# A chunked recurrence on TensorE: level products in 64*64 quarters, and as block-diagonal products of two heads

## The chip, the cores and the metric

The kernel runs on one core of a Trainium2 chip. The metric is the device time of one execution in microseconds; lower is better. All data are float32.

## The reference

Two layers of a hybrid backbone over 512 tokens (256 of context, 256 latent). Each layer normalises, projects, and mixes the tokens in three ways (RWKV-7 time mixing in both directions, neighbourhood attention, chunkwise mLSTM), merges the three, and then runs a mixture of experts. The part that matters here is the recurrence of the RWKV-7 mixer. It runs for each of 8 heads (64 channels each) and each of two directions over the tokens, with a 64 x 64 state S:

```python
def step(S, inp):
    r_t, w_t, a_t, b_t, k_t, v_t = inp
    sa = jnp.einsum('bhvk,bhk->bhv', S, a_t)
    S = S * w_t[:, :, None, :] + sa[..., None] * b_t[:, :, None, :] + v_t[..., None] * k_t[:, :, None, :]
    return S, jnp.einsum('bhvk,bhk->bhv', S, r_t)
```

The context tokens come first, and their last state starts the latent tokens. The second layer needs no outputs for the context tokens, only the state.

## The kernel before

The kernel is a chain of stages, each a block of its own in which the engines' programs are written out by hand and tied by semaphores; between stages all engines meet. `stage_rwkv_scan` (from L1824) does the recurrence, once in each layer. It moves nothing by DMA.

The 512 tokens are cut into chunks of L = 64, so there are NST = 8 steps, and in a step both directions d (0 and 1) work on a chunk each. P is 128, HD is 64, and KC = 4 pairs of heads fill the 128 partitions: an even head lies on partitions 0 to 63 and an odd one on 64 to 127. Within a chunk the recurrence is solved in closed form. TensorE makes the products of the decayed rows (`matrices`, L2149), a triangular matrix per head. Its inverse is built in six levels (m = 0 to 5), each of which joins blocks twice as large: a level multiplies the inverse so far, kept as X and as its transpose, by masked factors. In a level of the kernel before (`level`, L2166), `forward` (L2184) writes psW, which DVE masks into XI (`factor`, L2070), and `backward` (L2189) writes psWT, which ACT copies to NT (`copied`, L1930). Level 5 makes only the backward half, and DVE adds the identity (`inverse`, L2075).

Every product of a level is 64 x 64 of one head. The start partition of the operands and that of the output say in which quarter of the 128 x 128 array a product lies. Two of the four head pairs swap the halves of the partitions at each odd level, so that forward and backward products use all four quarters at once:

```python
def place(hp, r, m):
    return HD - r if hp >= KC // 2 and m % 2 else r
```

For that a level is issued in two halves with a wait on `across` in between (L2199 to L2201), and `between` (L2211) puts other products there: the right side from the state (L2220) and from the values (L2227), the turning of the features to token-major order by products with the identity (L2237), and at level 0 the old state's part of the output rows (L2268).

Behind the levels of a step, TensorE makes the next step's matrices (L2159 with 128 columns, L2162 with 64), the corrections u (L2247), the product that updates the state (L2254) and the chunk's part of the output rows (L2262), and then level 0 of the next step (`step`, L2272). DVE adds the state product to the old state (L2094) and multiplies by the chunk's decay (L2100); it also applies the masks to the matrices (L2068, L2088) and makes the queries (L2057, L2061). ACT takes the exponentials of the decay sums (four a direction and step, L1915 to L1918), copies the levels, the right side (L1945), the turned features (L1939), u (L1962, L1963) and the output rows (L1969). POOL makes the other features of the next step (L1988 to L1997) and clears the buffers at the start (L2003 to L2012). The values are transposed once at the start (L2146). In the program of each engine the two directions alternate, so one direction's copies run beside the other direction's products.

## Time and profile before

| | us |
|---|---|
| median of 3 runs | 2594.16 |
| lowest and highest run | 2587.97, 2595.68 |
| the profiled execution, its time | 2594.5 |
| its span, first to last instruction | 2592.7 |
| mean granted TensorE clock, share of full speed | 0.941 |

A page of the profile gives busy times by engine. PE is TensorE's products, PEld its weight loads, DVE is VectorE, ACT ScalarE, POOL GpSimd, SP SyncE. Views of the trace give single stretches: windows (busy times between two moments), waits, groups by source line, and the timeline. In the timeline a row of several records has the start of the first, the length from there to the end of the last, and their number. A row such as `64*64 64x64` has weights on 64 rows and 64 columns of the array, and moving data of 64 partitions and 64 columns. A record's length holds the way through the array, so successive records overlap; what one costs in a series is the distance of their starts. "issue" is time in which the engine waited for nothing that the profile shows.

### The profile page before, as it was taken

What the parts mean: (1) busy time and instruction counts of PE and PEld (TensorE: products, weight loads), DVE (VectorE), ACT (ScalarE), POOL (GpSimd) and SP (SyncE); (2) the same over time, 40 slices, a digit from 0 to 9 for tenths busy, and PEclk for the clock granted to TensorE, in tenths of its full rate; (3) what the DMA queues carried; (4) which work ended last, traced back from release to release, by engine and by line L of the source; (5) the groups of instructions that cost most, each with busy time, mean ns of one, the idle gap of its engine ahead of it and who ended that gap; (6) DMA issues with size and microseconds to landing.
All of it is one profiled execution on the core that took longest, in us unless ns stands there. A gap on an engine that the chain in (4) does not pass through costs nothing. (4 is left out here: it accounts for less than half of the span.)

```text
span 2592.7 us, 49039 instructions
## 1 busy us (share of the span) xinstructions
PE 2253.1 (87%) x19954; PEld 1492.5 (58%) x19954; DVE 1159.0 (45%) x2561; ACT 707.5 (27%) x1666; POOL 392.0 (15%) x465
## 2 busy tenths in 40 slices
PE   6999989887789998899889679999888878897785
PEld 3444455547754444466556568877657767554453
DVE  3877765575542114532212563244675542522113
ACT  2011155464441002132222120024454430222220
POOL 0000000044520001132222000000133400222210
PEclk8999999999999998999999889999889999899998
DMA  9455401210016103699988733313210033999994
GB/s 379 195 211 238 168 33 43 79 46 5 4 52 259 73 1 126 263 384 388 372 348 319 297 143 113 115 67 98 98 40 4 4 128 129 355 414 390 382 377 180
DMA packets 80368, 474.39 MB, mean 183 GB/s; under 512 B 17296, under 2 KB 29200, under 8 KB 51728
## 3 DMA queue, kind: packets, MB, share of 16 engines
q1 hardware_dynamic: 55280, 419.82, 41.3%
q0 software_dynamic: 24864, 51.43, 5.2%
q8 instruction: 159, 2.61, 0.4%
q14 instruction: 65, 0.53, 0.1%
HBM read 439.99 MB, written 61.08 MB: 193 GB/s over the span
## 5 line engine op out<-in xcount | busy, mean ns | idle before, releaser
L2883 PE MATMUL xp_psG<-moe_ring,rt_xt 128*64 128x256 f32 (+1 forms) x2048 | 324.5, 402 | 42.5 <-DMA moe_ring<-in_moe 41.9
L2883 PEld LDWEIGHTS xp_psG<-moe_ring,rt_xt 128*64 128x64 f32 (+1 forms) x2048 | 225.4, 161 | 119.6 <-issue 48.2
L599 PE MATMUL win_ps<-h,win_ring 128*128 128x512 f32 x512 | 226.2, 600 | 5.4 <-PEq L292 5.4
L659 DVE SCALAR_TENSOR_TENSOR mod_acc<-ada_ring,cv_silu,mod_acc 128x512 f32<-128x512 f32 x280 | 197.9, 748 | 10.8 <-issue 0.4
L3140 DVE TENSOR_TENSOR rt_sg<-rt_sg,xp_psG 128x128 f32<-128x128 f32 x84 | 24.2, 288 | 332.3 <-ACT rt_sg L2957 332.3
L599 PEld LDWEIGHTS win_ps<-h,win_ring 128*128 128x128 f32 x512 | 97.0, 192 | 125.6 <-issue 125.6
L2904 PE MATMUL xp_psY<-moe_ring,rt_aT 128*64 128x512 f32 (+1 forms) x512 | 162.1, 602 | 4.0 <-DVE rt_aT L3147 4.0
L2192 PE MATMUL sc_ps<-sc_NT,sc_XI 64*64 64x64 f32 x2560 | 112.9, 235 | 23.3 <-issue 18.9
L1274 POOL MEMSET ml_w<- 128x1536 f32 x4 | 5.4, 1376 | 764.9 <-POOLq L973 764.9
L2187 PE MATMUL sc_ps<-sc_XI,sc_NT 64*64 64x64 f32 x2048 | 100.7, 226 | 22.1 <-issue 16.6
L2073 DVE TENSOR_TENSOR sc_XI<-sc_ps,cst 128x256 f32<-128x256 f32 x160 | 67.5, 422 | 107.9 <-PE sc_ps L2192 107.0
L2951 ACT ACTIVATE rt_xt<-xp_psT 128x512 f32<-128x512 f32 x168 | 91.0, 595 | 89.8 <-PE xp_psT L2868 89.7
L2537 DVE TENSOR_TENSOR mg_gateb<-mg_gateb,mg_psY 128x512 f32<-128x512 f32 (+1 forms) x48 | 26.6, 554 | 189.6 <-PE mg_psY L2494 184.3
L2192 PEld LDWEIGHTS sc_ps<-sc_NT,sc_XI 64*64 64x64 f32 x2560 | 89.6, 142 | 28.7 <-issue 22.4
L2757 POOL DMA_INDIRECT y_rows<-rt_y,rt_dst x56 | 56.2, 1004 | 300.5 <-PE xp_psT L2868 197.6
L2957 ACT ACTIVATE rt_sg<-xp_psG 128x128 f32<-128x128 f32 x84 | 23.4, 279 | 265.1 <-PE xp_psG L2883 265.1
L2868 PEld LDWEIGHTS xp_psT<-cst,rt_xg 128*128 128x128 f32 x512 | 58.5, 144 | 64.4 <-issue 36.8
L2187 PEld LDWEIGHTS sc_ps<-sc_XI,sc_NT 64*64 64x64 f32 x2048 | 79.1, 137 | 27.7 <-issue 17.5
L1933 ACT ACTIVATE sc_NT<-sc_ps 128x256 f32<-128x256 f32 x160 | 61.3, 384 | 120.7 <-PE sc_ps L2192 120.5
L2904 PEld LDWEIGHTS xp_psY<-moe_ring,rt_aT 128*64 128x64 f32 (+1 forms) x512 | 51.7, 153 | 69.6 <-issue 59.9
L2868 PE MATMUL xp_psT<-cst,rt_xg 128*128 128x128 f32 x512 | 70.7, 283 | 21.5 <-DMA rt_xg<-h_rows,rt_tok 21.5
L2508 PE MATMUL mg_psO<-mg_m,mg_wo 128*128 128x512 f32 (+1 forms) x256 | 83.0, 486 | 4.2 <-DVE mg_m L2541 4.2
(537 smaller groups left out, 4293.4 us busy)
## 6 DMA issues: line engine op xcount, KB each, us to landing
moe_ring<-in_moe SPq DMA_DIRECT2D x128, 1536.0 KB, 14.3
ada_ring<-in_ada SPq DMA_DIRECT2D x22, 2048.0 KB, 15.1
win_ring<-in_win SPq DMA_DIRECT2D x20, 2048.0 KB, 7.8
cb_yg<-y_rows SPq DMA_DIRECT2D x16, 1024.0 KB, 11.6
mg_ring<-in_mg SPq DMA_DIRECT2D x16, 768.0 KB, 4.4
mg_wo<-in_wo SPq DMA_DIRECT2D x2, 4096.0 KB, 14.5
pr<-y_rows SPq DMA_DIRECT2D x8, 1024.0 KB, 18.4
ml_gate_ring<-in_mg SPq DMA_DIRECT2D x12, 512.0 KB, 3.7
```

What stands on the lines that cost most here:

```text
L599: last = pe.matmul(ps[:, n % NB, first(n):T], ring[:, j % 2, c, m * P:(m + 1) * P], h[:, c, first(n):T], start=c == 0, stop=c == KD - 1)
L659: last = dve.scalar_tensor_tensor(out=acc[:, a % 2, s], in0=aring[:, a % 3, c], scalar=weight, in1=acc[:, a % 2, s], op0=ALU.mult, op1=ALU ...
L1933: act.activation(NT[d][:], psWT[d], ACT.Copy).then_inc(sem[d]["wtout"].sem, 1)
L2073: dve.tensor_tensor(XI[d][:], psW[d], level_mask(d, m), ALU.mult).then_inc(sem[d]["xi"].sem, 1)
L2187: pe.matmul(psW[d][to:to + HD, hp], wt, x, start=True, stop=True)
L2192: last = pe.matmul(out[to:to + HD], x, wt, start=True, stop=True)
L2508: last = pe.matmul(psO[:, m % 2, 0:N], wo[:, c, m * P:(m + 1) * P], mg[:, c, t0:T], start=c == 0, stop=c == KD - 1)
L2757: pool.indirect_dma_start(k.d_y[0:N * TOP_K], bass.IndirectOffsetOnAxis(ap=dst[:, column(u)], axis=0), y_rows[u % OUT], None, bounds_check ...
L2868: last = pe.transpose(psT[:, u % 2, c], xg[u % AHEAD][:, c * P:(c + 1) * P], k.cst("ident"))
L2883: last = pe.matmul(psG[at:at + m, u % 2, 0:2 * P].rearrange("p (q n) -> p q n", q=2), xt[:, u % 2, c, at:at + m], ring[:, slot, c:2 * KD:K ...
L2904: last = pe.matmul(psY[at:at + m, q], aT[:, u % 2, at:at + m], ring[:, slot, 2 * KD + 4 * q:2 * KD + 4 * q + 4], start=True, stop=True)
L2951: last = act.activation(xt[:, u % 2, q * 4:q * 4 + 4], psT[:, u % 2, q * 4:q * 4 + 4], ACT.Copy)
```

## The change

The levels from 1 up work on two heads at once. NT becomes a block-diagonal [128, 4, 2, 64]: the even head's block on partitions 0 to 63, the odd head's on 64 to 127, the rest zero, cleared once by POOL. A level is then, for each of the four pairs of heads, one product with XI as weights (128 rows, 64 columns) and NT as 128 moving columns ("back", psWT, rows 0 to 63), and one with NT as 128 x 128 weights and XI as 64 moving columns (psW, called "forward" below). Each back result is copied by two instructions, `evens` and `odds`, mostly on ACT, some on DVE (`both`, `odds_of_first`). X0 and the matrices M now hold all heads' level operands on partitions 0 to 63, so level 0 uses two quarters. The matrices are one product of 128 x 128 outputs a head, into banks of their own (psA), and are made during level 4 and not behind level 5; the second matrices (psA2) go around level 5. Token-major order comes from full transposes. The identity's part of the inverse and the old state are added by products with the identity as weights, in place of DVE adds; the sum S2 and its buffer go. ACT takes two exponentials a direction and step and not four. The products of the right side, the output rows and the state keep their shapes, and their places in the order change; `rows_of_state` now opens the sum of the output rows.

The diff, cut to its core:

```diff
-        S2 = sb("S2", [P, KC, L])
-        ex = sb("ex", [P, 3, KC, L])
+        rise = sb("rise", [P, KC, L])
+        fall = [sb(f"fall{b}", [P, KC, L + 1]) for b in range(3)]
...
-        NT = sb("NT", [P, KC, L])
-        XI = sb("XI", [P, KC, L])
-        X0 = ctx.enter_context(nc.sbuf_tensor(f"sc_X0{l}", [P, 2, KC, L], F32))
+        NT = [[pn[:, NK_T + 2 + 2 * b + d].rearrange("p (c o n) -> p c o n", c=KC, o=2) for d in range(2)] for b in range(2)]
+        XI = [pn[:, NK_T + 6, d * KC * L:(d + 1) * KC * L].rearrange("p (c n) -> p c n", c=KC) for d in range(2)]
+        X0 = ctx.enter_context(nc.sbuf_tensor(f"sc_X0{l}", [HD, 2, HEADS, L], F32))
...
-        psA = [ps[d][:, 0:2].rearrange("p b (h n) -> p b h n", n=P) for d in range(2)]
         psW = [half(d, 0, 0) for d in range(2)]
-        psWT = [half(d, 1, 0) for d in range(2)]
-        psA2 = [half(d, 3, 1) for d in range(2)]
-        psV = [ps[d][:, 2].rearrange("p (c n) -> p c n", c=KC) for d in range(2)]
-        psBK = [[half(d, 2, o) for o in range(2)] for d in range(2)]
-        psI = [ps[d][:, 0:2, 0:2 * L].rearrange("p b (c n) -> p b c n", c=KC // 2) for d in range(2)]
-        psR = [half(d, 3, 0) for d in range(2)]
+        psA2 = [ps[d][0:HD, 0].rearrange("p (h n) -> p h n", h=HEADS) for d in range(2)]
+        psWT = [ps[d][:, 1].rearrange("p (c o n) -> p c o n", c=KC, o=2) for d in range(2)]
+        psWT0 = [half(d, 1, 0) for d in range(2)]
+        psV = [ps[d][:, 1] for d in range(2)]
+        psA = [ps[d][:, 2:4].rearrange("p b (h n) -> p b h n", n=P) for d in range(2)]
+        psBK = [ps[d][:, 2] for d in range(2)]
         psU = [half(d, 2, 0) for d in range(2)]
         psS = [half(d, 2, 1) for d in range(2)]
+        psR = [half(d, 3, 0) for d in range(2)]
...
-            incl, excl, total = sums[:, :, 1 - d:1 - d + L], sums[:, :, d:d + L], sums[:, :, L - d * L]
-            act.activation(ex[d][:, 2], incl, ACT.Exp, scale=DECAY)
-            act.activation(ex[d][:, 0], incl, ACT.Exp, scale=-DECAY)
-            act.activation(ex[d][:, 1], excl, ACT.Exp, scale=-DECAY)
-            act.activation(wl[n % 3][d][:], total, ACT.Exp, scale=-DECAY).then_inc(sem[d]["exps"].sem, 1)
+            act.activation(rise[d][:], sums[:, :, 1 - d:1 - d + L], ACT.Exp, scale=DECAY)
+            act.activation(fall[n % 3][d][:], sums, ACT.Exp, scale=-DECAY).then_inc(sem[d]["exps"].sem, 1)
...
-        def copied(d, n, m):
-            w(act, d, "nn", n, m + 1)
-            act.activation(NT[d][:], psWT[d], ACT.Copy).then_inc(sem[d]["wtout"].sem, 1)
+        def evens(d, n, m):
+            w(act, d, "back", n, m + 1)
+            src = psWT0[d][0:HD] if m == 0 else psWT[d][0:HD, :, 0]
+            act.activation(NT[m % 2][d][0:HD, :, 0], src, ACT.Copy).then_inc(sem[d]["evens"].sem, 1)
+        def odds(d, n, m):
+            w(act, d, "back", n, m + 1)
+            src = psWT0[d][HD:P] if m == 0 else psWT[d][0:HD, :, 1]
+            act.activation(NT[m % 2][d][HD:P, :, 1], src, ACT.Copy).then_inc(sem[d]["odds"].sem, 1)
         def token_major(d, n):
             w(act, d, "turned", n)
-            for o in range(2):
-                last = act.activation(bk[d][:, o:HEADS:2], psBK[d][o], ACT.Copy)
-            last.then_inc(sem[d]["tok"].sem, 1)
+            act.activation(bk[d][:].rearrange("p h n -> p (h n)"), psBK[d], ACT.Copy).then_inc(sem[d]["tok"].sem, 1)
...
         def step(n):
             for m in range(1, 5):
-                for d in range(2):
-                    copied(d, n, m)
-                    if n == 0 and m == 1:
-                        exponentials(d, 1)
-                    if m == 2:
-                        right_side(d, n)
-                    if m == 4:
-                        token_major(d, n)
+                evens(0, n, m)
+                odds(0, n, m)
+                if m == 2:
+                    token_major(0, n)
+                if m == 4:
+                    right_side(1, n)
+                if n == 0 and m == 1:
+                    exponentials(0, 1)
+                    exponentials(1, 1)
+                if m % 2:
+                    evens(1, n, m)
+                    odds(1, n, m)
+                if m == 2:
+                    token_major(1, n)
+                if m == 3:
+                    right_side(0, n)
             if n + 2 < NST:
                 exponentials(0, n + 2)
+            evens(0, n, 5)
+            odds(0, n, 5)
+            evens(1, n, 5)
+            odds(1, n, 5)
...
+            if n + 1 < NST:
+                evens(0, n + 1, 0)
+                odds(0, n + 1, 0)
+                evens(1, n + 1, 0)
...
+        blocks = pn[:, NK_T + 2:NK_T + 6]
+        pool.memset(blocks, 0.0)
...
-                    pool.tensor_copy(X0[:, d], eye)
+                    pool.tensor_copy(X0[:, d], k.cst("eye", HD).unsqueeze(1).broadcast_to([HD, HEADS, L]))
...
+            w(dve, d, "seconds", n, 2)
+            first = k.cst(f"lev{d}", HD)[:, 0:L].unsqueeze(1).broadcast_to([HD, HEADS, L])
+            dve.copy_predicated(X0[:, d], first.bitcast(U32), psA2[d]).then_inc(sem[d]["xi"].sem, 1)
...
-        def inverse(d, n):
-            w(dve, d, "nn", n, 6)
-            dve.tensor_tensor(NT[d][:].rearrange("p (b c) n -> p b c n", b=2), psI[d],
-                              eye.rearrange("p (b c) n -> p b c n", b=2), ALU.add).then_inc(sem[d]["inv"].sem, 1)
+        def odds_of_first(d, n):
+            w(dve, d, "back", n)
+            dve.tensor_copy(NT[0][d][HD:P, :, 1], psWT0[d][HD:P]).then_inc(sem[d]["odds"].sem, 1)
+        def both(d, n, m):
+            w(dve, d, "back", n, m + 1)
+            dve.tensor_copy(NT[m % 2][d][0:HD, :, 0], psWT[d][0:HD, :, 0]).then_inc(sem[d]["evens"].sem, 1)
+            dve.tensor_copy(NT[m % 2][d][HD:P, :, 1], psWT[d][0:HD, :, 1]).then_inc(sem[d]["odds"].sem, 1)
...
-        def add_products(d, n):
+        def decay(d, n):
             w(dve, d, "s", n)
-            dve.tensor_tensor(S2[d][:], S[d][:], psS[d], ALU.add)
-        def decay(d, n):
-            if n in outs:
-                w(dve, d, "rows", n)
-            dve.tensor_tensor(S[d][:], S2[d][:], wl[n % 3][d][:].unsqueeze(2).broadcast_to([P, KC, L]),
+            total = fall[n % 3][d][:, :, L - d * L]
+            dve.tensor_tensor(S[d][:], psS[d], total.unsqueeze(2).broadcast_to([P, KC, L]),
                               ALU.mult).then_inc(sem[d]["state"].sem, 1)
         def step(n):
+            more = n + 1 < NST
             for m in range(1, 5):
-                for d in range(2):
-                    factor(d, n, m + 1)
-                if n + 1 < NST:
+                factor(0, n, m + 1)
+                if m % 2 == 0:
+                    both(1, n, m)
+                factor(1, n, m + 1)
+                if more:
                     (rows_query if m % 2 else key_query)((m - 1) // 2, n + 1)
-            for d in range(2):
-                inverse(d, n)
-            if n + 1 < NST:
+            if more:
+                masks(0, n + 1)
+            if more:
+                masks(1, n + 1)
                 for d in range(2):
                     first_factor(d, n + 1)
-                    masks(d, n + 1)
-            for d in range(2):
-                add_products(d, n)
-            dve.drain()
-            for d in range(2):
-                decay(d, n)
-                if n + 1 < NST:
+                odds_of_first(1, n + 1)
+                for d in range(2):
                     factor(d, n + 1, 1)
-            dve.drain()
+                for d in range(2):
+                    decay(d, n)
+                dve.drain()
...
         def matrices(d, n):
             w(pe, d, "queries", n)
             w(pe, d, "feats", n)
             if n:
-                w(pe, d, "inv", n - 1)
+                w(pe, d, "tok", n - 1)
                 w(pe, d, "rout", n - 1)
             for h, hp, r in heads:
-                o = h % 2
-                for a, q in enumerate((r, HD - r)):
-                    pe.matmul(psA[d][q:q + HD, o, hp], hat[n % 2][d][r:r + HD, hp, a],
-                              ra[n % 2][d][r:r + HD, hp].rearrange("p a n -> p (a n)"), start=True, stop=True)
+                last = pe.matmul(psA[d][:, h % 2, hp], hat[n % 2][d][r:r + HD, hp].rearrange("p a n -> p (a n)"),
+                                 ra[n % 2][d][r:r + HD, hp].rearrange("p a n -> p (a n)"), start=True, stop=True)
+            last.then_inc(sem[d]["mats"].sem, 1)
+        def second_matrices(d, n, o):
+            if o:
+                w(pe, d, "seconds", n)
+            r = o * HD
+            for hp in range(KC):
+                last = pe.matmul(psA2[d][:, 2 * hp + o], ra[n % 2][d][r:r + HD, hp, 1], hat[n % 2][d][r:r + HD, hp, 0],
+                                 start=True, stop=True)
+            last.then_inc(sem[d]["seconds"].sem, 1)
+        def first_level(d, n):
+            w(pe, d, "xi", n)
+            w(pe, d, "masked", n)
+            if n:
+                w(pe, d, "evens", n - 1, 6)
+                w(pe, d, "odds", n - 1, 6)
+            else:
+                pe.wait_ge(values_out.sem, values_out.at(NV))
             for h, hp, r in heads:
-                last = pe.matmul(psA2[d][r:r + HD, hp], ra[n % 2][d][r:r + HD, hp, 1], hat[n % 2][d][r:r + HD, hp, 0],
+                last = pe.matmul(psWT0[d][r:r + HD, hp], X0[:, d, h], M[n % 2][d][0:HD, h % 2, hp, L:P],
                                  start=True, stop=True)
-            last.then_inc(sem[d]["mats"].sem, 1)
+            last.then_inc(sem[d]["back"].sem, 1)
+            for h, hp, r in heads:
+                last = pe.matmul(psW[d][r:r + HD, hp], M[n % 2][d][0:HD, h % 2, hp, L:P], X0[:, d, h],
+                                 start=True, stop=True)
+            last.then_inc(sem[d]["nn"].sem, 1)
         def level(d, n, m):
             w(pe, d, "xi", n, m + 1)
...
+            w(pe, d, "evens", n, m)
+            w(pe, d, "odds", n, m)
+            if m == 5 and n + 1 < NST:
+                second_matrices(d, n + 1, 0)
+            wt = NT[(m - 1) % 2][d]
+            for hp in range(KC):
+                last = pe.matmul(psWT[d][0:HD, hp], XI[d][:, hp], wt[:, hp], start=True, stop=True)
+            last.then_inc(sem[d]["back"].sem, 1)
             if m < 5:
+                for hp in range(KC):
+                    last = pe.matmul(psW[d][:, hp], wt[:, hp], XI[d][:, hp], start=True, stop=True)
+                last.then_inc(sem[d]["nn"].sem, 1)
...
+        def token_major(d, n):
+            w(pe, d, "state", n)
+            for hp in range(KC):
+                last = pe.transpose(psBK[d][:, hp * P:(hp + 1) * P],
+                                    hat[n % 2][d][:, hp].rearrange("p a n -> p (a n)"), k.cst("ident"))
+            last.then_inc(sem[d]["turned"].sem, 1)
+        def side_of_state(d, n):
+            w(pe, d, "state", n)
+            pe.wait_ge(sem[d]["yout"].sem, sem[d]["yout"].at(y_read(n)))
             for h, hp, r in heads:
+                last = pe.matmul(psR[d][r:r + HD, hp], ra[n % 2][d][r:r + HD, hp, 1], S[d][r:r + HD, hp],
+                                 start=hp == 0, stop=False)
+            last.then_inc(sem[d]["rstate"].sem, 1)
+        def side_of_values(d, n):
+            w(pe, d, "rstate", n)
             for h, hp, r in heads:
+                last = pe.matmul(psR[d][r:r + HD, hp], M[n % 2][d][HD:P, h % 2, hp, L:P],
+                                 uv[HD:P, chunk(d, n), h], start=False, stop=hp == KC - 1)
+            last.then_inc(sem[d]["r"].sem, 1)
         def rows_of_state(d, n):
             if n in outs:
                 for h, hp, r in heads:
                     last = pe.matmul(psY[d][r:r + HD, hp], S[d][r:r + HD, hp], ra[n % 2][d][r:r + HD, hp, 0],
+                                     start=hp == 0, stop=False)
+                last.then_inc(sem[d]["ystate"].sem, 1)
+        def corrections(d, n):
+            w(pe, d, "rout", n)
+            if n + 1 < NST:
+                w(pe, d, "masked", n + 1)
+            else:
+                w(pe, d, "tok", n)
+            rows_of_state(d, n)
+            w(pe, d, "evens", n, 6)
+            w(pe, d, "odds", n, 6)
+            pe.matmul(psU[d], k.cst("ident"), rhs[d][:], start=True, stop=False)
+            for hp in range(KC):
+                last = pe.matmul(psU[d][:, hp], NT[1][d][:, hp], rhs[d][:, hp], start=False, stop=hp == KC - 1)
+            last.then_inc(sem[d]["u"].sem, 1)
+        def state_product(d, n):
+            w(pe, d, "uout", n)
+            if n + 1 < NST:
+                pe.matmul(psS[d], k.cst("ident"), S[d][:], start=True, stop=False)
+                for h, hp, r in heads:
+                    last = pe.matmul(psS[d][r:r + HD, hp], bk[d][:, h], uv[:, chunk(d, n), h],
+                                     start=False, stop=hp == KC - 1)
+                last.then_inc(sem[d]["s"].sem, 1)
+            if n in outs:
+                w(pe, d, "ystate", n)
+                for h, hp, r in heads:
+                    last = pe.matmul(psY[d][r:r + HD, hp], uv[:, chunk(d, n), h], M[n % 2][d][:, h % 2, hp, 0:L],
                                      start=False, stop=hp == KC - 1)
                 last.then_inc(sem[d]["rows"].sem, 1)
         def step(n):
+            for m in range(1, 5):
                 for d in range(2):
                     level(d, n, m)
+                    if m == 1:
+                        token_major(d, n)
+                    elif m == 2:
+                        side_of_state(d, n)
+                    elif m == 3:
+                        side_of_values(d, n)
+                    elif n + 1 < NST:
+                        matrices(d, n + 1)
             for d in range(2):
+                level(d, n, 5)
                 if n + 1 < NST:
+                    second_matrices(d, n + 1, 1)
+            for d in range(2):
                 corrections(d, n)
+            if n + 1 < NST:
+                for d in range(2):
+                    first_level(d, n + 1)
             for d in range(2):
                 state_product(d, n)
```

## Rows read from the trace of the kernel before

**Rows 1.** The page: its first line and the busy times of its part 1.
```profile
span 2592.7 us, 49039 instructions
...
PE 2253.1 (87%) x19954; PEld 1492.5 (58%) x19954; DVE 1159.0 (45%) x2561; ACT 707.5 (27%) x1666; POOL 392.0 (15%) x465
```

**Rows 2.** Windows: start:end, length, busy (records) of five engines, clock, DMA, GB/s.
```profile
564.20:750.95 186.75, 146.76 (x5648) 135.62 (x5648) 99.91 (x222) 83.01 (x256) 92.97 (x133) 0.94 0.02 4
577.40:750.95 173.55, 136.82 (x5476) 126.79 (x5472) 89.36 (x197) 75.68 (x235) 84.59 (x119) 0.96 0.02 4
1916.30:2099.80 183.50, 146.96 (x5392) 134.63 (x5392) 98.49 (x222) 80.97 (x248) 76.86 (x109) 0.88 0.02 4
1934.10:2099.80 165.70, 136.12 (x5228) 124.95 (x5220) 88.75 (x197) 72.37 (x223) 69.22 (x95) 0.91 0.02 4
```

**Rows 3.** Waits, first scan: who waited for what, us, times, longest.
```profile
ACT sc_NT L1933 <- PE sc_ps L2192: 57.4, 56, 2.7
DVE sc_XI L2073 <- PE sc_ps L2192: 54.8, 55, 2.6
...
PE sc_ps L2192 <- issue: 11.8, 11, 1.6
...
PE sc_ps L2187 <- issue: 9.1, 8, 1.9
```

**Rows 4.** Groups by line, first scan: count, busy, mean ns, idle before.
```profile
L2073 DVE TENSOR_TENSOR sc_XI<-sc_ps,cst 128x256 f32<-128x256 f32 x80 | 33.8, 422 | 55.2 <-PE sc_ps L2192 54.8
L1933 ACT ACTIVATE sc_NT<-sc_ps 128x256 f32<-128x256 f32 x80 | 30.6, 384 | 57.5 <-PE sc_ps L2192 57.4
```

**Rows 5.** Timeline of PE, first scan: start, length, line, shapes, count.
```profile
606.74 0.69 PE L2237 MATMUL sc_ps<-cst,sc_hat 64*64 64x64 f32 x32
```

**Rows 6.** Timeline of PE, end of the second step of the first scan.
```profile
615.57 1.06 PE L2159 MATMUL sc_ps<-sc_ra,sc_hat 64*64 64x128 f32 x30
...
616.91 0.65 PE L2247 MATMUL sc_ps<-sc_rhsb,sc_NT 64*64 64x64 f32 x16
617.49 0.69 PE L2254 MATMUL sc_ps<-sc_uv,sc_bk 128*64 128x64 f32 x16
618.01 0.64 PE L2262 MATMUL sc_ps<-h,sc_uv 128*64 128x64 f32 x16
618.47 0.64 PE L2254 MATMUL sc_ps<-sc_uv,sc_bk 128*64 128x64 f32 x16
618.94 0.64 PE L2262 MATMUL sc_ps<-h,sc_uv 128*64 128x64 f32 x16
619.51 0.27 PE L2187 MATMUL sc_ps<-sc_X,h 64*64 64x64 f32 x2
```

**Rows 7.** Timeline of PE, attention stage.
```profile
379.64 1.90 PE L1137 MATMUL na_psO<-vna,na_pt 128*128 128x64 f32 x16
381.38 1.04 PE L1125 MATMUL na_psT<-cst,na_s 128*128 128x128 f32 x8
```

**Rows 8.** Timeline of PE, stage ahead of the first scan.
```profile
519.82 4.46 PE L247 MATMUL rf_psG<-h,rf_gate_ring 128*128 128x512 f32 x10
524.21 1.99 PE L1803 MATMUL rf_ps<-pr,rf_lw 64*128 64x512 f32 x8
526.13 5.42 PE L247 MATMUL rf_psG<-h,rf_gate_ring 128*128 128x512 f32 x12
531.48 0.70 PE L1803 MATMUL rf_ps<-pr,rf_lw 64*128 64x512 f32 x2
```

**Rows 9.** Timeline of PE, stage behind the second scan.
```profile
2103.32 1.89 PE L2408 MATMUL ro_psV<-ro_sq,cst 128*128 128x256 f32 x8
```

**Rows 10.** Timeline of POOL and of DVE, start of the second scan.
```profile
1916.32 1.81 POOL L2003 MEMSET h<- 128x2048 f32 x1 [28.63 <-POOLq L1593]
1918.08 0.98 POOL L2006 COPY sc_X<-cst 128x256 f32<-128x256 f32 x2
...
1929.50 0.45 DVE L2068 COPY_PREDICATED sc_X<-cst,sc_ps 128x256 f32<-128x256 uint32 x1 [6.16 <-POOL scratch L2012]
```

151 lines of the change are left out of this document (31 added, 120 removed).

## The prediction, made before the changed kernel was run

> **What bounds the kernel now.** I began with the page: TensorE is busy 87% of the span, DVE 45%, ACT 27% [rows 1]. That says little about the part that changes, so I cut the span into stretches. The scan runs twice, 186.75 us in the first layer and 183.50 us in the second; without the start-up, which ends with level 0 of the first step, the eight steps take 173.55 and 165.70 us [rows 2], so 21.7 and 20.7 us a step. Almost no DMA runs there (share 0.02), so nothing outside competes, and what the stages gain or lose goes into the span at full size. In that stretch DVE is busy for 89.4 us, ACT for 75.7, POOL for 84.6 and PE for 136.8: PE is the fullest, but not full.
>
> The waits say why [rows 3]. ACT and DVE wait for the level products, as they should. PE itself waits little for them; its largest gaps are "issue", 11.8 and 9.1 us at the two level lines alone, up to 1.9 us each. So a step is TensorE work plus some exposed latency and gaps.
>
> How much TensorE work? A source product in float32 is two records (each of the eight-product groups shows x16). Per step and direction the source has: levels 1 to 4, 16 products each; level 5, 8; level 0, 16; both parts of the right side, 8 and 8; token-major, 16; matrices, 16 and 8; corrections, state product, and the two output parts, 8 each. That is 176, so 704 records a step for both directions; times 8, plus 16 transposes of the values at one record each, 5648, exactly the count in the first stretch [rows 2].
>
> Their price depends on where they lie in the array. 32 products of 64*64 that go to all four quarters take 0.69 us: (0.69 - 0.22) / 31 = 0.015 us a record [rows 5]. 16 that use two quarters take 0.65: (0.65 - 0.22) / 15 = 0.029 [rows 6]. So a quarter is done with 64 columns in 0.058 us, whatever the others do. The levels, matrices and token-major use four quarters, the others two. Per direction: levels 128 + 32 + 16 records and 32 of token-major at 0.015 = 3.1; the first matrices 32 with 128 columns at 0.026 = 0.8 (below); the other 112 records at 0.029 = 3.2. Two directions: 14.4 us of the 21.7. About 7 us a step are latency, gaps and half clock (granted 0.96 and 0.91, [rows 2]). That is all that fewer or better placed instructions could win.
>
> **The change, by its prices.** Full-width products cost more each, and rows elsewhere in the trace have them.
> - 128*128 weights with 64 columns: (1.90 - 0.22) / 15 = 0.112 us [rows 7]. The 64 columns would be done in 0.055; the wide weight load sets the pace.
> - 512 columns: from 519.82 to 524.21 ten records take 4.39, so 0.43 each, and 256 columns (1.89 - 0.38) / 7 = 0.216 [rows 8, 9]. By this line 128 columns cost 0.11. The 128-column matrices agree: 30 in four quarters take 1.06 us, (1.06 - 0.32) / 29 = 0.026 each, so 0.10 in a quarter [rows 6].
> - Going from one shape of the array to another costs too. From 524.21 to 526.13 eight records of 64*128 work in pairs, 4 x 0.43 = 1.72, and take 1.92: 0.20 more. From 526.13 to 531.48 twelve records take 5.35 against 5.16, again 0.2 [rows 8]. From 617.49 to 619.51 the 64 records of 128*64 take 2.02, against 64 x 0.029 = 1.86 [rows 6]. So each entry costs 0.20 us with 128-wide weights and 0.15 with 64-wide ones.
>
> **The sum for one step, both directions.**
> - Levels 1 to 4, eight of them. "Back" has 128*64 weights, 128 columns, and writes rows 0 to 63 only, so its products share a column half and follow one another: 8 records x 0.11 + 0.15 = 1.03. "Forward" (psW) has block-diagonal 128*128 weights, 64 columns: 8 x 0.112 + 0.20 = 1.10. 2.13 a level, 17.0 in all. Before, a level was 32 records at 0.015, half a microsecond. This is the step on which everything rests.
> - Token-major: 8 transposes, one record each, 0.11: 0.9.
> - Right side from state and from values: 4 groups of 16 x 0.029 + 0.15: 2.5.
> - Matrices: 2 x (8 pairs x 0.11 + 0.20) = 2.2. As dear as before: half the products, each twice as wide.
> - Second matrices: 32 records, each group of 8 in one quarter, so 0.058 each, 1.9, and level 5 "back", 16 x 0.11 = 1.8; five entries, 0.75: 4.4.
> - Corrections: old-state rows 32 x 0.029, identity of 256 columns 4 x 0.216, block-diagonal 16 x 0.112, entries 0.55: 4.1.
> - Level 0 of the next step, two quarters: 64 x 0.029 + 0.15 = 2.0.
> - State product: per direction identity 2 x 0.216 + 0.20, then 32 x 0.029 + 0.15: 3.4.
>
> 36.5 us a step. The last step has no next matrices (2.2 + 1.9 + 0.6 of entries), no level 0 (2.0) and no state part (2.2): 27.7. In the second layer the first four steps write no rows, 2.0 us less each. First layer: 7 x 36.5 + 27.7 = 283.2; second: 4 x 34.5 + 3 x 36.5 + 27.7 = 275.2. Before: 173.6 + 165.7. **Loss: 219.1 us.**
>
> **What lies beside it at no cost.** ACT (9.5 us a step by [rows 2]) gets nine more copies a step of 0.38 us and four fewer exponentials, DVE (11.2) five more copies of about 0.42 and four fewer adds [rows 4]; each stays near 12 us against 36 of PE. A level's two copies follow "back" while "forward" runs, and the mask multiply (0.42) runs while the other direction's level takes 2.1 us. If that cover were gone, a level would show about 1 us of wait. State updates and the copies of u lie under the other direction's corrections and level 0. Removed at DVE are the identity add and the S2 add; both were off the path there. Only the last step has them bare, 1 us a layer. DVE's new wait for the second matrices has only later mask work behind it, with 4 us of corrections to cover it.
>
> Start-up: POOL clears 2048 more columns (1.81) and its identity copies double (0.98 more); DVE already waited 6.16 us for POOL in the second layer [rows 10]. I take 3 us there and 1 us in the first, between 0 and 6.
>
> Sum: 2594.5 (the profiled execution, 2592.7 of span and 1.8 around it; the median is 2594.2) + 219.1 + 4 + 2 = 2820 us.
>
> A rule weighed against the rows. Ten records in a row with 128*128 weights take 0.43 us each for 512 columns, and eight take 0.216 for 256 [rows 8, 9]: half the columns, half the time, so no load shows. The Trainium skill, TensorE: Matmul & The Clock Gate, section The mechanism, says that a weight load overlaps running matmuls only if its row group differs. By that rule no full-height product would hide its load, and the sum would come out higher, as in the second rival below.
>
> **The rivals.**
> - *Entries are hidden (2727).* Counted above are about 5.9 us of entries a step. Were they free, 16 x 5.9 = 93 us less. For: they might fall into waits. Against: PE has no waits left. 8%.
> - *Loads are not hidden in one tile (about 3010).* A 128-wide load is 0.11 us if it is what sets the pace in [rows 7]; I take half for 64. Each record of "back" then pays 0.055 more (80 a step, 4.4), each wide one with 64 columns 0.05 (80, 4.0), the 8 transposes and 8 identity records 1.8, the 32 of the second matrices 1.8: 12 a step, 192 us. Against: [rows 7 to 9]. This is what the Trainium skill's rule above would give. 3%.
> - *Gaps and half clock stay (2880).* The issue gaps shrink only with the records, 464 for 704: 2 x 20.9 x 0.66 = 28 us; and 5% at half clock, 28 us more. For: both are there now [rows 2, 3]. Against: the records now come at a third of the density, and PE has no pauses. 9%.
> - *Faster (about 2490).* Time goes by records and not by columns: 464 x 0.029 = 13.5, with the rest of latency 15 us a step, 16 x 6.7 = 107 us less. It decides at the average record: below 21.7 / 464 = 0.047 us the change wins. For: 34% fewer records, PE's gaps are "issue". Against: 0.112 in [rows 7]. 3%.
> - *It does not do what it says:* a forgotten dependence serialises the directions again, or nothing changes. 1% for no change; a longer chain falls in the range.
>
> **How the numbers follow.** My forecast has 76%, with its own range 2785 to 2860 (price errors of a tenth on 36.5 us a step make 58 us, errors of one sign throughout are unlikely, and forgotten waits only add). The range for 8 in 10 reaches towards cheaper entries and towards remaining gaps: 2760 to 2890. A change of less than 0.3%, 8 us, can't be told from none. Slower has 0.96, same 0.01, faster 0.03.
>
> **What the profile after should show.** 3692 and 3436 PE records in the two scans; steps of about 36 us; "back" records 0.11 apart, "forward" 0.112, with a pause of 0.2 between the groups; PE busy above 95% of the stages; the granted clock near 1.00; DVE and ACT waiting longer for PE, issue gaps almost gone. Wrong would be: a step under 25 us, records with 64 columns at 0.06, or PE waiting for ACT's copies.

## The result, and the profile after

The changed kernel takes 2834.53 us, the median of 4 runs (2831.64 to 2839.77), against 2594.92 for the kernel before (4 runs beside it, 2587.97 to 2598.2). The ratio is 1.093, 95% interval 1.0901 to 1.0958: 240 us slower. The forecast was 2820 us, a loss of about 226. The profiled execution took 2831.64 us, its span is 2829.8; in [rows 1] the span was 2592.7.

The page after, first line and busy times of part 1:

```profile
span 2829.8 us, 41305 instructions
...
PE 2537.5 (90%) x16042; PEld 1724.3 (61%) x16042; DVE 1174.9 (42%) x2573; ACT 752.0 (27%) x1698; POOL 394.6 (14%) x467
```

7734 instructions fewer than in [rows 1] (3912 records of products and as many weight loads go, a few operations of other engines come), and TensorE is busy 284 us longer. A count of instructions would have pointed the wrong way.

The windows of after: the first scan whole and without its start-up, then the second scan likewise (columns as in [rows 2]).

```profile
569.00:868.06 299.06, 288.77 (x3692) 252.64 (x3693) 107.75 (x228) 105.12 (x272) 95.08 (x134) 0.98 0.01 2
581.50:868.06 286.56, 277.21 (x3554) 242.99 (x3550) 96.57 (x204) 98.03 (x258) 84.62 (x119) 0.99 0.01 2
2032.50:2333.11 300.61, 283.97 (x3436) 248.09 (x3437) 105.61 (x229) 102.05 (x264) 77.88 (x110) 0.96 0.01 2
2056.00:2333.11 277.11, 268.64 (x3284) 235.26 (x3285) 94.06 (x202) 94.81 (x249) 67.98 (x95) 0.99 0.01 2
```

Against [rows 2] the two scans grew by 112 and 117 us, 229 of the 237 between the two spans; the other 8 are small differences of stages that the change does not touch (4.8 ahead of the first scan, 3.8 behind the second). The steps of the first scan last 36.5 us, the last two 36.1, and one of them, the second below, 39.5, for a part of it ran at the lower level of the clock. In the kernel before a step is 22.4 by the same measure (experiment 4).

```profile
615.39:651.86 36.47, 35.26 (x468) 30.92 (x465) 12.81 (x28) 12.51 (x35) 7.29 (x10) 1.00 0.01 2
651.86:691.36 39.50, 38.28 (x468) 33.42 (x464) 13.08 (x28) 12.52 (x35) 11.52 (x16) 0.91 0.01 2
```

The timeline of TensorE over one step of after (start, length, line, shapes, records; lengths overlap, so read starts against starts):

```profile
640.78 1.16 PE L2178 MATMUL sc_ps<-sc_ra,sc_hat 64*128 64x128 f32 x16 [1.21 <-DVE sc_ra L2079]
641.87 0.68 PE L2188 MATMUL sc_ps<-sc_hat,sc_ra 64*64 64x64 f32 x8
642.48 1.09 PE L2219 MATMUL sc_ps<-pn 128*64 128x128 f32 x8
...
646.30 0.70 PE L2269 MATMUL sc_ps<-sc_rhsb,cst 128*128 128x256 f32 x2
646.84 1.00 PE L2271 MATMUL sc_ps<-sc_rhsb,pn 128*128 128x64 f32 x8
647.77 0.68 PE L2255 MATMUL sc_ps<-pn,sc_S 64*64 64x64 f32 x16
...
651.86 0.70 PE L2278 MATMUL sc_ps<-sc_S,cst 128*128 128x256 f32 x2
652.49 0.69 PE L2280 MATMUL sc_ps<-sc_uv,sc_bk 128*64 128x64 f32 x16
...
656.15 1.10 PE L2223 MATMUL sc_ps<-pn 128*128 128x64 f32 x8
657.09 0.61 PE L2230 MATMUL sc_ps<-cst,sc_hat 128*128 128x128 f32 x4
657.63 1.09 PE L2219 MATMUL sc_ps<-pn 128*64 128x128 f32 x8
658.64 1.10 PE L2223 MATMUL sc_ps<-pn 128*128 128x64 f32 x8
...
662.79 1.09 PE L2219 MATMUL sc_ps<-pn 128*64 128x128 f32 x8
663.80 1.10 PE L2223 MATMUL sc_ps<-pn 128*128 128x64 f32 x8
664.84 0.68 PE L2239 MATMUL sc_ps<-sc_S,sc_ra 64*64 64x64 f32 x16
```

A level is "back" at 662.79 and "forward" at 663.80, over at 664.84: 2.05 us, where half a microsecond did it before. Eight such levels a step are most of the loss (experiment 10). The first row holds what the forecast did not have: TensorE stands for 1.21 us and waits for VectorE.

The waits in the first scan of after (waiting engine and line, releaser, us in total, times, longest):

```profile
ACT pn L1929 <- PE sc_ps L2219: 144.0, 63, 7.9
...
DVE pn L2092 <- PE sc_ps L2223: 96.5, 64, 2.2
```

In [rows 3] ACT waited 57.4 us and DVE 54.8 for the level products. They wait longer, since TensorE is the slow one now, and of the issue gaps that stood there nothing of size is left.

### The profile page after: what moved, and what is told of

It reads as the page before. It is cut to its first block and busy times, and to the rows that moved or that the text cites. A ratio compares the mean times of both kernels' runs of the same rounds, so it can differ in the third digit from the quotient of the medians.

```text
span 2829.8 us, 41305 instructions
## 1 busy us (share of the span) xinstructions
PE 2537.5 (90%) x16042; PEld 1724.3 (61%) x16042; DVE 1174.9 (42%) x2573; ACT 752.0 (27%) x1698; POOL 394.6 (14%) x467
## 5 line engine op out<-in xcount | busy, mean ns | idle before, releaser
L2219 PE MATMUL sc_ps<-pn 128*64 128x128 f32 x1280 | 177.3, 283 | 0.7 <-DVE pn L2092 0.5
L2219 PEld LDWEIGHTS sc_ps<-pn 128*64 128x64 f32 x1280 | 139.1, 139 | 14.9 <-issue 5.5
L2092 DVE TENSOR_TENSOR pn<-sc_ps,cst 128x256 f32<-128x256 f32 x160 | 66.5, 424 | 196.0 <-PE sc_ps L2223 195.5
L1929 ACT ACTIVATE pn<-sc_ps 64x256 f32<-64x256 f32 x160 | 60.3, 377 | 318.1 <-PE sc_ps L2219 298.5
L2223 PE MATMUL sc_ps<-pn 128*128 128x64 f32 x1024 | 142.3, 282 | 0.0
L2223 PEld LDWEIGHTS sc_ps<-pn 128*128 128x128 f32 x1024 | 124.7, 192 | 22.2 <-issue 22.2
L2895 PE MATMUL xp_psT<-cst,rt_xg 128*128 128x128 f32 x512 | 70.9, 284 | 25.6 <-DMA rt_xg<-h_rows,rt_tok 25.5
```

What stands on the lines that cost most here:

```text
L1929: act.activation(NT[m % 2][d][0:HD, :, 0], src, ACT.Copy).then_inc(sem[d]["evens"].sem, 1)
L2092: dve.tensor_tensor(XI[d][:], psW[d], level_mask(d, m), ALU.mult).then_inc(sem[d]["xi"].sem, 1)
L2219: last = pe.matmul(psWT[d][0:HD, hp], XI[d][:, hp], wt[:, hp], start=True, stop=True)
L2223: last = pe.matmul(psW[d][:, hp], wt[:, hp], XI[d][:, hp], start=True, stop=True)
L2895: last = pe.transpose(psT[:, u % 2, c], xg[u % AHEAD][:, c * P:(c + 1) * P], k.cst("ident"))
```

## The experiments

All runs are of the whole kernel. "After" is the changed kernel, and "the step" is the distance from one state product to the next.

**1 to 3. Doubling one group of products.** The duplicates write the same values again.

```
 back_again_128:  after line 2219, the same loop once more
 back_again_64:   after line 2219, once more with the first 64 columns only
+                    for hp in range(KC):
+                        last = pe.matmul(psWT[d][0:HD, hp, 0], XI[d][:, hp], wt[:, hp, 0], start=True, stop=True)
 forward_again:   after line 2223, the same loop once more
```

> The changed kernel, in which the back products of levels 1 to 5 are issued a second time into the same place: 8 more records of 128*64 weights and 128 columns behind each of the 160 groups. Theory (TensorE is full, and a record costs what its columns or its load take): the new records stand 0.11 us apart, 16 x 10 x 8 x 0.11 = 141 us, so about 2975 us. Rival 1 (time goes by the number of records, 36.5 us for 464 of them, 0.08 each): 100 us, 2935. Rival 2 (TensorE is not what sets the time; copies and waits do): under 20 us, 2850.

> The changed kernel, in which behind each group of back products the even half (64 of the 128 columns) is issued again with the same weights: as many new records as in back_again_128, with half the columns. Theory: 64 columns and a load of 64 take 0.058 us where a record follows another in the same part of the array, 16 x 10 x 8 x 0.058 = 74 us, so about 2908 us, half the price of back_again_128. Rival 1 (records count, not columns): the same as back_again_128. Rival 2 (waits set the time): under 20 us.

> The changed kernel, in which the forward products of levels 1 to 4 (128*128 block-diagonal weights, 64 columns) are issued a second time: 8 more records behind each of 128 groups. Theory: the load of 128 columns of weights sets the pace, 0.112 us a record as in the attention stage, 128 x 8 x 0.112 = 115 us, so about 2949 us. Rival (the 64 moving columns set the pace, 0.058): 59 us, about 2893. Rival 2 (waits set the time): under 20 us.

Measured: 2963.83 us (ratio to before 1.1427, 1.1404 to 1.145), 2901.57 (1.1178, 1.1151 to 1.1205) and 2956.43 (1.1425, 1.1342 to 1.1508). Over after that is 129, 67 and 122 us, where theory had 141, 74 and 115. The 122 is a middle value and no run's: the four runs of forward_again are 2934.31 and 2936.29 (granted clock 0.953 and 0.952), and 2976.58 and 2976.57 (0.936 and 0.940), so about 101 or 142 over after. Either is well above the 59 of the rival. The profile is of the first pair. The timeline of TensorE in back_again_64, one level, with the added group at L2221:

```profile
663.68 1.09 PE L2219 MATMUL sc_ps<-pn 128*64 128x128 f32 x8
664.60 0.63 PE L2221 MATMUL sc_ps<-pn 128*64 128x64 f32 x8
665.16 1.10 PE L2225 MATMUL sc_ps<-pn 128*128 128x64 f32 x8
```

The same in forward_again, with the added group at L2225:

```profile
664.73 1.10 PE L2223 MATMUL sc_ps<-pn 128*128 128x64 f32 x8
665.67 1.06 PE L2225 MATMUL sc_ps<-pn 128*128 128x64 f32 x8
```

The added back group with 64 columns takes 0.56 us with the change of shape behind it, 67 us in all (0.052 a record); the one with 128 columns 129 (0.101). The same number of records with half the columns costs half: time goes by columns here and not by records, so the rival "faster" is out. With 128*128 weights 64 columns cost about 0.11 each by the timeline (0.90 to 0.94 us for eight), as 128 columns with 64-wide weights do. Twice the width of the weights doubles the price beside 64 columns, so the load sets the pace there. Both prices of the forecast stand: 0.101 for 0.11 and 0.052 for 0.058 a record, and for the wide weights about 0.11 by the timeline for 0.112.

**4. before_levels_again.** In the kernel before, each product of levels 1 to 4 is issued twice.

```
-                            pe.matmul(psW[d][to:to + HD, hp], wt, x, start=True, stop=True)
+                            for _ in range(2 if 0 < m < 5 else 1):
+                                pe.matmul(psW[d][to:to + HD, hp], wt, x, start=True, stop=True)
...
-                            last = pe.matmul(out[to:to + HD], x, wt, start=True, stop=True)
+                            for _ in range(2 if 0 < m < 5 else 1):
+                                last = pe.matmul(out[to:to + HD], x, wt, start=True, stop=True)
```

> The kernel before, in which every product of levels 1 to 4 is issued twice in a row: 32 more records of 64*64 for each of 128 levels, 4096 in all, four times as many as in forward_again. Theory (four quarters work at once, 0.015 us a record where all four are fed): 4096 x 0.015 = 61 us, less what falls into waits that are there, so 2625 to 2655 us. If the packing into quarters were worth nothing (0.029 to 0.058 a record), 119 to 238 us, 2714 to 2833; if the kernel before is bound by instruction supply, the gaps called issue grow with the records (by half, some 20 us) on top of the 61.

Measured: 2706.61 us (1.0439, 1.0418 to 1.0461), 112 more for 4096 records, 0.027 us each and not 0.015. **The expectation missed.** Windows over six step periods of the first scan of the kernel before:

```profile
594.54:729.20 134.66, 106.51 (x4226) 98.86 (x4224) 71.14 (x157) 56.91 (x176) 70.66 (x100) 0.95 0.02 4
```

The windows of this kernel over the same periods:

```profile
598.91:775.64 176.73, 135.96 (x5763) 126.44 (x5760) 70.15 (x158) 57.46 (x176) 70.35 (x99) 1.00 0.02 5
```

TensorE's busy time grows by 29.4 us for 1537 records, 0.019 each, a little more at an equal clock (0.95 and 1.00); the rest, 12.6 us, is time in which it does nothing. The waits of this kernel name it, over the whole first scan:

```profile
PE sc_ps L2194 <- issue: 17.9, 18, 1.6
PE sc_ps L2188 <- issue: 14.8, 16, 1.5
```

These were 11.8 and 9.1 in [rows 3]. The last clause of the expectation comes nearest, though its 81 us are too few as well. 4226 records in 134.66 us are 31.4 a microsecond, 5763 in 176.73 are 32.6: nearly the same, with a third more records. It suggests that the kernel before is bounded, in its scans, partly by how fast records arrive; no run shows it. I take that up again in the last section.

**5. query_first.** VectorE's query operation goes ahead of the factor of level 5.

```
                         factor(0, n, m + 1)
+                        if more and m == 4:
+                            key_query(1, n + 1)
                         if m % 2 == 0:
                             both(1, n, m)
                         factor(1, n, m + 1)
-                        if more:
+                        if more and m < 4:
                             (rows_query if m % 2 else key_query)((m - 1) // 2, n + 1)
```

> The kernel after, with VectorE's second query operation for the reverse direction (line 2079) issued ahead of the level's factor instead of behind it; no work is added or left out. In the kernel after TensorE stands about 1.3 us each step ahead of the next matrices of the second direction, four waits for that line adding to 5.1 us in a scan. Theory (that wait is the one the forecast missed): each of the 14 steps with a successor becomes 1.2 to 1.3 us shorter, 2834.5 - 17 = about 2817 us, and the step period goes from 36.1-36.5 to about 35.1. Rival (a wait that only moves: the factor or the copy behind the query is then late by as much): within 4 us of 2834.5, and the waits show level 5 waiting for VectorE.

Measured: 2812.86 us (1.0848, 1.0822 to 1.0874), 22 less. The step is 35.20 in place of 36.49. Six periods of after, then six of this kernel, in which TensorE is busy for the whole of the window:

```profile
616.01:837.21 221.20, 214.63 (x2785) 188.06 (x2785) 77.54 (x163) 73.96 (x195) 73.66 (x104) 0.98 0.01 2
609.03:820.24 211.21, 211.21 (x2786) 185.56 (x2786) 75.34 (x163) 73.98 (x195) 73.05 (x104) 1.00 0.01 2
```

The wait is real, and nothing took its place. It is not the whole of the 22 us. The row of those who wait for the query in after sums it over both scans:

```profile
PE sc_ps L2178: 15.2, 14
```

Behind two of these 14 waits, those that end at 677.27 and 2079.14, the granted clock of after falls to 0.50 for some microseconds; the first time this makes the step of 39.50 us, 3.0 too long. In the scans of query_first, once their start-up is over, the clock stays at 1.00 throughout. Whether the waits bring the lower clock about is not shown: twelve of them have none behind them.

**6. back_wide.** The back products get the shape of the forward ones. XB is the buffer in which XI lies, taken 128 columns wide at each pair of heads, so the upper half of the weights is the next pair's factor or zeros; rows 64 to 127 that the products write are read by nobody.

```
-  last = pe.matmul(psWT[d][0:HD, hp], XI[d][:, hp], wt[:, hp], start=True, stop=True)
+  last = pe.matmul(psWT[d][:, hp], XB[d][:, hp * L:hp * L + P], wt[:, hp], start=True, stop=True)
```

> The kernel after, with the back products of levels 1 to 5 given weights 128 columns wide (the neighbouring head pair's block or zeros stand in the upper half), so that they write all 128 rows and have the same 128*128 shape as the forward products; the rows 64 to 127 that they write are read by nobody. As many records, as many columns. Theory (an entry into another array shape costs about 0.1 us and the first load of a group shows): the entry between back and forward goes, 8 times per step and a part of those at level 5; about 0.15 to 0.25 us for each of some 9 places, 1.4 to 2.2 us a step, 2834.5 - (22 to 36) = 2800 to 2812 us. Rival 1 (shape changes cost nothing, the gap is the wait for VectorE or the drain of the group): within 4 us. Rival 2 (a wider load sets the pace of a 128-column product): each back record goes from 0.109 towards 0.16, 80 records a step, 4 us a step, about 2900 us.

Measured: 2804.3 us (1.0812, 1.0788 to 1.0837), 30 less. One level in its timeline:

```profile
652.60 1.06 PE L2220 MATMUL sc_ps<-pn 128*128 128x128 f32 x8
653.49 1.00 PE L2224 MATMUL sc_ps<-pn 128*128 128x64 f32 x8
654.33 0.61 PE L2231 MATMUL sc_ps<-cst,sc_hat 128*128 128x128 f32 x4
```

Back takes 0.89 us and forward 0.84, where after had 1.01 and 0.95 (657.63 to 659.59). This level lies between the transposes, of the same shape, and so loses both changes; next to the products of 64*64 back stays at 1.0 and only forward gains (0.93 for 1.04). As many columns, as many records, wider loads, and yet faster: changing the shape of the array costs about 0.1 us each time. A load twice as wide beside 128 columns costs nothing. The step is 35.08, 1.41 less, which makes some 20 of the 30 us; of the rest the step of 39.50 us, which this profile does not have, is 3, and the others were not followed.

**7. wide_and_query**, the edits of 5 and 6.

> The two edits together: VectorE's second query operation for the reverse direction goes ahead of the level's factor, and the back products have weights 128 columns wide. Nothing is left out. Each alone took 1.29 and 1.41 us off the step of 36.49; with the wide weights 0.9 us a step of wait for the query remained. Theory (two separate losses): what remained of the wait goes, 2804.3 - 14 x 0.9 = about 2792 us, a step of 34.2 us. Rival (both edits removed the same stall): within 4 us of 2804.

Measured: 2793.48 us (1.0767, 1.0746 to 1.0789), a step of 34.11. Two separate losses, 41 us together. The two alone sum to 52, but in back_wide the wait was already down to 0.9 us, and a stretch at the lower clock can be saved only once.

**8. copies_again.** Each of ACT's copies of the back products is made twice, with a drain between; the same edit in evens.

```
                     src = psWT0[d][HD:P] if m == 0 else psWT[d][0:HD, :, 1]
+                    act.activation(NT[m % 2][d][HD:P, :, 1], src, ACT.Copy)
+                    act.drain()
                     act.activation(NT[m % 2][d][HD:P, :, 1], src, ACT.Copy).then_inc(sem[d]["odds"].sem, 1)
```

> The kernel after, with each of ScalarE's copies of the back products made twice, a drain between: 19 copies of about 0.38 us and 19 drains more on ScalarE in each step, 7 to 9 us on top of its 11 to 12, of a step of 36. Theory (the copies lie under forward and under the other direction's level): within 8 us of 2834.5. Rival (the copies are on the chain, back to copy to the next level): two copies in a row for each of ten levels a step, 0.4 to 0.8 us each, 4 to 8 us a step, 2900 us or more.

Measured: 2833.02 us (1.0923, 1.0894 to 1.0953), no change against after. The extra work went into ACT's wait for the back products. In the first scan it was 144.0 us in after; the waits of copies_again show:

```profile
ACT pn L1929 <- PE sc_ps L2223: 97.4, 63, 7.0
```

ScalarE makes 19 such copies a step, so 19 more were hidden, with their drains. The nine that the change adds cost nothing.

**9. before_state_identity.** In the kernel before, the old state is added by an identity product and not by VectorE.

```
-                    dve.tensor_tensor(S[d][:], S2[d][:], wl[n % 3][d][:].unsqueeze(2).broadcast_to([P, KC, L]),
+                    dve.tensor_tensor(S[d][:], psS[d], wl[n % 3][d][:].unsqueeze(2).broadcast_to([P, KC, L]),
...
-                        add_products(d, n)
-                    dve.drain()
-                    for d in range(2):
+                        w(dve, d, "s", n)
                         decay(d, n)
...
                     w(pe, d, "uout", n)
+                    pe.matmul(psS[d], k.cst("ident"), S[d][:], start=True, stop=False)
```

> The kernel before with one part of the change alone: the old state is added by one identity product per direction into the state product's bank, and VectorE's add of it goes, with the drain behind the two adds. Theory by the forecast's prices (four records of 256 columns at 0.216 us and two entries of 0.2 us, 1.3 us a step, with the add of 0.42 us off TensorE's path): up to 1.3 us for each of 16 steps, 2594.3 + 15 to 21 = 2609 to 2615 us. Rival (the add and the drain stood on the path from the state product to the next step's sides): 0.4 to 0.9 us a step come back, and the time is within 8 us of 2594.3.

Measured: 2601.91 us (1.0029, 1.0012 to 1.0046), 3 to 12 us more. Theory's 15 is outside, the rival's bound of 8 inside the interval. The product costs something and part of it falls into gaps that TensorE has anyway; how much the add gave back was not separated. As a part of the 240 us it is small.

**10. levels_four_quarters.** Levels 1 to 5 alone go back to products of one head, on the block-diagonal storage; evens are read from rows 64 to 127 of the bank. Cut to the new loop:

```
+                    for hp in range(KC):
+                        for o, r in ((0, 0), (1, HD)):
+                            q = HD - r
+                            last = pe.matmul(psWT[d][q:q + HD, hp, o], XI[d][r:r + HD, hp], wt[r:r + HD, hp, o],
+                                             start=True, stop=True)
+                            if m < 5:
+                                ahead = pe.matmul(psW[d][r:r + HD, hp], wt[r:r + HD, hp, o], XI[d][r:r + HD, hp],
+                                                  start=True, stop=True)
```

> The kernel after with levels 1 to 5 alone put back to products of one head: 16 products of 64*64 back and 16 forward with 64 columns each, taken in turn so that all four quarters of the array are used, in place of 8 block-diagonal products each way. Everything else of the change stays: matrices in own banks, masks, identity products, block-diagonal corrections. Theory (the loss sits in the levels, by price of the block-diagonal products): a level 1 to 4 costs 64 records at 0.015 = 0.96 us and an entry instead of 1.96 to 2.05, level 5 0.93 instead of 1.02, so 8 x 1.05 = 8.4 us a step, 16 steps: 2834.5 - 134 = about 2700 us, a step of 28 to 29 us; well over half of the 240 us comes back. Rival 1 (the shorter levels lay bare the copies and the mask): 0.4 to 0.8 us of wait for each of eight levels, 51 to 102 us less gained, 2750 to 2800 us, and the waits name ACT and DVE. Rival 2 (the levels are not the cause): above 2810.

Measured: 2642.51 us (1.0187, 1.0165 to 1.0209). The direction is as expected, the size is not: 192 us come back and not 134. The slip is in my text: a level has 8 products of one head each way, not 16, so 32 records and 0.48 us. (The forecast's "32 products of 64*64" are 32 records too; its sum counts them rightly.) With that, 8 levels save about 1.4 us each and the two of level 5 about 0.5 each; less 0.6 for a wait that grew (experiment 11) this is about 12 a step, and 16 steps give the 192. The six periods from 600.40 to 749.32 are 148.92 us, 24.8 a step. One level in the windows of after:

```profile
660.10:662.15 2.05, 2.05 (x17) 1.81 (x16) 0.70 (x2) 0.85 (x3) 1.14 (x2) 1.00 0.00 0
```

A level of the same code as here in the windows of levels_and_query, 32 records and two of its neighbours:

```profile
655.90:656.54 0.64, 0.64 (x34) 0.56 (x32) 0.00 (x0) 0.64 (x3) 0.00 (x0) 1.00 0.00 0
```

Twice the records, under a third of the time. Four fifths of the loss are the block-diagonal levels.

**11. levels_and_query**, with the query ahead of the factor as well (the edit of experiment 5 on that of 10).

> As levels_four_quarters, with VectorE's second query operation for the reverse direction ahead of the level's factor as well. Theory: the wait ahead of the next matrices is larger once the levels are short, since VectorE's row of work per level stays, and moving the query takes 1.3 us or more off each of 14 steps: 18 us or more below levels_four_quarters, about 2680 us. Rival (VectorE and ScalarE set the pace of the short levels, so the order does not matter): within 5 us of levels_four_quarters.

Measured: 2609.2 us (1.0064, 1.0043 to 1.0085), 33 less than levels_four_quarters, so the order matters and the rival is out. (The 2680 of the expectation rests on the 2700 that experiment 10 missed.) In levels_four_quarters the waits show that the one for the query had grown to 1.9 us a step, 25.5 us over both scans; what else the 33 hold was not followed:

```profile
PE sc_ps L2178 <- DVE pn L2079: 7.2, 4, 1.9
```

**12. quarters_throughout.** The rest at full width goes into quarters too. The edit of the corrections, on levels_and_query, stands below. The state's identity product is split in the same way, level 5 issues one of the next second matrices ahead of each pair of its own products, the transposes of both directions follow level 1 of the second one, and the memset of the blocks goes.

```
-                    pe.matmul(psU[d], k.cst("ident"), rhs[d][:], start=True, stop=False)
-                    for hp in range(KC):
-                        last = pe.matmul(psU[d][:, hp], NT[1][d][:, hp], rhs[d][:, hp], start=False, stop=hp == KC - 1)
+                    for r in (0, HD):
+                        pe.matmul(psU[d][r:r + HD], k.cst("ident")[r:r + HD, r:r + HD], rhs[d][r:r + HD], start=True, stop=False)
+                    for h, hp, r in heads:
+                        last = pe.matmul(psU[d][r:r + HD, hp], NT[1][d][r:r + HD, hp, h % 2], rhs[d][r:r + HD, hp],
+                                         start=False, stop=hp == KC - 1)
```

> levels_and_query, with what else of the change works at full width or in one quarter brought into quarters: the identity products of the corrections and of the state as two products of 64*64 with 256 columns each side by side, the corrections by one product a head, the first half of the next second matrices between the products of level 5, the transposes of both directions one behind the other, and no clearing of the blocks that now are never read. Nothing is left out. By rows of levels_and_query: the corrections of a direction fall from 1.6 to about 0.95 us (1.3 us a step), the state's identity products by 0.2 each (0.4), level 5 with the second matrices by 0.43 each (0.8), one return from the transposes' shape (0.3), clearing 1.8 us a scan: 2609.2 - (16 x 1.3 + 14 x 1.5 + 3.5) = 2564 us. Theory (full-width shapes are what the rest of the loss consists of; the new order and banks are sound): 2555 to 2580 us, below the kernel before. Rival (steps of 22 us are set by latency and issue gaps, as in the kernel before, and not by TensorE's work): above 2590 us, with the gaps in the waits grown by what the products gave up.

Measured: 2571.76 us, median of 6 (2568.0 to 2576.24), ratio 0.9911, 0.989 to 0.9931: 23 us faster than the kernel before. The corrections of one direction in its timeline:

```profile
653.14 0.60 PE L2278 MATMUL sc_ps<-sc_rhsb,cst 64*64 64x256 f32 x4
653.58 0.63 PE L2280 MATMUL sc_ps<-sc_rhsb,pn 64*64 64x64 f32 x16
654.04 0.63 PE L2263 MATMUL sc_ps<-pn,sc_S 64*64 64x64 f32 x16
```

Its windows over six step periods:

```profile
597.47:718.53 121.06, 117.99 (x3795) 104.46 (x3793) 76.54 (x163) 74.52 (x196) 74.42 (x103) 1.00 0.02 4
```

The corrections take 0.90 us, in after 1.47 (646.30 to 647.77). A step is 20.2 us over six periods, in the kernel before 22.4 by the window in experiment 4. TensorE's *busy* time went up from 106.5 to 118.0; what fell is its idle time, from 28.2 to 3.1 us. So this kernel wins over the one before with 431 records fewer in those six periods, without the issue gaps, and at a full clock (1.00 for 0.95). The parts of this run were not tried one by one.

## Why the prediction was right, point by point

- **The block-diagonal levels: right.** The sum had 2.13 us a level, the trace has 2.05 between products of 64*64 and 1.96 between the transposes. Back was priced 1.03 and measured 1.01 to 1.02; forward was priced 1.10 and measured 0.94 to 1.04. The term that was too large is the entry into 128-wide weights with 64 columns, 0.20 in the sum and about 0.1 here (experiment 6). Experiment 10 shows that the levels are the cause.
- **The other terms: right in size.** The corrections were priced at 4.1 us a step and take 4.2 (645.69 to 649.85), of it 0.54 for an identity pair and 0.93 for a block-diagonal group. The state's identity pair takes 0.63 (651.86 to 652.49), as summed. The matrices take 1.09 each, as summed.
- **"PE has no pauses": wrong.** One wait of up to 1.2 us a step (15.2 us in 14 steps) stood ahead of the next matrices of the reverse direction. The second query operation of VectorE (line 2079) is queued behind the factor of level 5, and that behind the product that TensorE has just done. The timeline of VectorE in after shows it: the factor (L2092), then the query (L2079), which starts at 676.42 and takes 0.79 us; TensorE's matrices start at 677.27, 1.22 us after it ran out of work. I looked at what each engine's load is and at the waits that the change adds, not at the order in which VectorE serves two consumers. Without it the kernel is 22 us faster (experiment 5); the cheaper forward entries, some 0.1 us eight times a step, 13 us in all, took more than half of it back. That the sum for the scans (225 us with start-up and last steps) came within 4 us of the measured 229 is owed in part to luck: these two errors stand against each other, and so do those of the start-up: the forecast had 1 us more in the first scan and 3 in the second, and measured were 0.7 less and 5.7 more (12.50 for 13.20, 23.50 for 17.80).

```profile
676.08 0.42 DVE L2092 TENSOR_TENSOR pn<-sc_ps,cst 128x256 f32<-128x256 f32 x1 [0.17 <-PE sc_ps L2223]
676.42 0.79 DVE L2079 SCALAR_TENSOR_TENSOR pn<-kkn,sc_fall 128x256 f32<-128x256 f32 x1
```

- **ACT and VectorE at no cost: right** for ACT's copies (experiment 8), wrong for VectorE's query. VectorE's other work was not doubled in any run; behind the start-up of the first scan TensorE waits for it 0.5 us in all, once.
- **Counts: right.** 3692 and 3436 records, as summed; steps of 36.5 in the first scan and 34.5 in the second where no rows are written.
- **Clock: right.** The stages without start-up show 0.99 against 0.96 and 0.91 in [rows 2]; what is missing from 1.00 are start-up's end and the two stretches of experiment 5.
- **The rivals.** "Entries are hidden" fell by experiment 6. "Loads are not hidden in one tile" fell by experiments 1 and 6: a second back group costs 0.101 us a record with 128 columns and 0.052 with 64, so no load of fixed length is in it. The Trainium skill's rule on row groups (TensorE: Matmul & The Clock Gate, The mechanism), by which that load would show, does not hold for these float32 products; the same section names a second way for a load to go ahead, into a background buffer for weights, and the measured times fit that one. "Gaps and half clock stay" fell: no issue gap of size is left in the scans of after, and two short stretches at the lower clock. "Faster" fell by experiments 1 and 2.

## What to carry to other kernels

Before two small products become one block-diagonal product, compare the time in the array and not the instruction count: four quarters side by side did 32 records in 0.48 us, 16 records at full width took 2.05 for the same products, and half of what they multiplied was zeros. Keep neighbours in one shape, or pay about 0.1 us at each change. When a step is rearranged, write down for the engine that serves two consumers which of its operations comes first: an operation queued one place too late was worth some 17 to 22 us (experiment 5), and is found in one line of the waits.

## What was not expected of the hardware

- **Three kernels with small records have nearly the same rate of them.** 31.4 records a microsecond in the kernel before, 32.6 with its levels doubled, 31.3 (3795 in 121.06 us) in quarters_throughout; the array did 32 records of a level in 0.48 us, twice that rate. In the second scan the kernel before shows 31.3, by its windows over the periods there:

```profile
1949.66:2095.96 146.30, 119.49 (x4579) 109.43 (x4577) 78.17 (x175) 62.37 (x190) 58.71 (x82) 0.91 0.02 4
```

  and the one with its levels doubled 33.3:

```profile
2013.79:2205.03 191.24, 150.51 (x6371) 139.22 (x6368) 78.14 (x175) 62.75 (x191) 58.25 (x82) 0.99 0.02 4
```

  Pauses of up to 1.9 us marked "issue" appear in the kernel before and in the one with its levels doubled, and hardly any at 26.7 (levels_and_query, 3650 records in 136.45 us). A limit on the supply of instructions would give this picture, but it is argued from these rates and not shown; no run changed the rate alone. Two things speak against a plain limit on the mean rate: quarters_throughout runs at 31.3 with 3.1 us idle in six periods, and one scan reaches 33.3. A rival was not tested: the kernel before issues each level in two halves with a wait and other products between them, and quarters_throughout does not.
- **A wider load is free beside 128 columns** and sets the pace beside 64 (experiments 3 and 6).
- **Two identity products of 64*64 with 256 columns side by side** take 0.44 us (653.14 to 653.58), as much as the one at 128*128 by the forecast's price (2 x 0.216); the 0.54 that the latter took in after (646.30 to 646.84) holds a change of shape as well.
